# Weight slots handed on as they come free, turns amid the next pair's products, and the last two expert pairs combined on TensorE

## The reference, cut to what matters

```python
N_EXPERTS = 32; TOP_K = 2; D_EXPERT = 256; D = 1024      # 256 tokens

# router: one group of 8 experts per token, then the best two in it
w_top = softmax(top_logit) * p_grp
combine = one_hot(g_sel)[:, :, None] * w_exp[:, None, :]
for grp in range(4):                                      # 8 experts each
    hid = silu(einsum('td,edf->tef', t, w_gate[grp])) * einsum('td,edf->tef', t, w_up[grp])
    out = out + einsum('tef,efd->td', hid * combine[:, grp, :, None], w_down[grp])
h = h + m[5] * out
return rmsnorm(h, final_norm_g)
```

## Time and profile before

| | us |
|---|---|
| time, median of 3 runs | 2303.52 (2302.74 to 2309.55) |
| the profiled execution's own time | 2301.17 |
| its span | 2299.2 |
| PE busy in the span | 2061.1 (90%) |
| DVE busy | 787.0 (34%) |
| ACT busy | 500.0 (22%) |
| POOL busy | 125.1 (5%) |

### The profile page before, as it was taken

One profiled execution on the slowest core, in us unless ns is written; L12 is line 12 of the kernel. 1 busy time (PEld: TensorE's weight loads), 2 busy tenths in 40 slices (PEclk: granted clock), 3 DMA queues, 4 the chain that ended last, 5 costly groups with the idle time before them and its releaser, 6 DMA issues. The chain is left out here.

```text
span 2299.2 us, 35930 instructions
## 1 busy us (share of the span) xinstructions
PE 2061.1 (90%) x15698; PEld 1271.5 (55%) x15698; DVE 787.0 (34%) x1613; ACT 500.0 (22%) x1023; POOL 125.1 (5%) x127
## 2 busy tenths in 40 slices
PE   6989999999999999999998887899998996778874
PEld 3545568854445658864544786884498643322221
DVE  1474323211185323310244545436444412311112
ACT  2223321201114413210121332123332201211111
POOL 0000000000000000000000011000021000011111
PEclk9999999999999999999998888889989998899997
DMA  6351325533343236334211000100200262387873
GB/s 253 146 206 54 147 110 219 220 146 146 127 186 139 105 122 257 147 147 157 99 44 42 3 3 3 49 12 37 110 4 3 74 265 110 146 360 325 342 325 154
DMA packets 33978, 318.47 MB, mean 139 GB/s; under 512 B 7088, under 2 KB 9528, under 8 KB 12960
## 3 DMA queue, kind: packets, MB, share of 16 engines
q1 hardware_dynamic: 28064, 308.40, 34.1%
q0 software_dynamic: 5760, 7.78, 1.0%
HBM read 332.49 MB, written 13.65 MB: 151 GB/s over the span
## 5 line engine op out<-in xcount | busy, mean ns | idle before, releaser
L516 ACT ACTIVATE arena<-pair 128x512 f32<-128x512 f32 (+5 forms) x339 | 181.0, 547 | 694.7 <-PE pair L890 172.7
L1267 PE MATMUL pair<-arena,weight_ring 128*128 128x256 f32 x1408 | 311.0, 383 | 2.9 <-ACT arena L790 2.9
L890 PE MATMUL pair<-weight_ring,arena 128*128 128x512 f32 (+1 forms) x640 | 279.2, 590 | 19.2 <-issue 11.4
L1267 PEld LDWEIGHTS pair<-arena,weight_ring 128*128 128x128 f32 x1408 | 270.0, 192 | 43.9 <-issue 6.8
L890 PEld LDWEIGHTS pair<-weight_ring,arena 128*128 128x128 f32 x640 | 123.5, 196 | 157.2 <-issue 151.9
L1313 PE MATMUL pair<-weight_ring,arena 128*128 128x512 f32 x352 | 151.5, 592 | 3.1 <-DVE arena L1287 3.1
L1287 DVE SCALAR_TENSOR_TENSOR arena<-pair,columns,arena 128x255 f32<-128x255 f32 (+1 forms) x176 | 76.8, 478 | 202.3 <-ACT arena L1278 200.7
L2777 PE MATMUL pair<-arena 128*64 128x512 f32 x352 | 111.5, 651 | 24.8 <-DMA arena<-experts_in 24.8
L2777 PE MATMUL pair<-weight_ring,arena 128*64 128x512 f32 x288 | 96.1, 657 | 22.9 <-DMA weight_ring<-experts_in 18.4
L1313 PEld LDWEIGHTS pair<-weight_ring,arena 128*128 128x128 f32 x352 | 66.8, 190 | 86.7 <-issue 83.2
L1573 PEld LDWEIGHTS pair<-arena 64*64 64x64 f32 x3584 | 111.1, 139 | 3.6 <-issue 2.9
(11 more groups left out here) (487 smaller groups left out, 2580.2 us busy)
## 6 DMA issues: line engine op xcount, KB each, us to landing
weight_ring<-stream SPq DMA_DIRECT2D x85, 2048.0 KB, 7.3
arena<-experts_in SPq DMA_DIRECT2D x18, 2048.0 KB, 13.2
weight_ring<-experts_in SPq DMA_DIRECT2D x14, 2048.0 KB, 12.4
arena<-experts_out SPq DMA_DIRECT2D x8, 2048.0 KB, 14.2
weight_ring<-experts_out SPq DMA_DIRECT2D x8, 2048.0 KB, 15.4
weight_ring<-stream SPq DMA_DIRECT2D x4, 1024.0 KB, 4.7
arena<-rows_in SPq DMA_DIRECT2D x1, 3264.0 KB, 21.9
weight_ring<-stream SPq DMA_DIRECT2D x2, 1152.0 KB, 5.5
```

Source lines behind the costliest of these rows:

```text
L516: copy_act = lambda dst, src: nc.scalar.activation(dst, src, ACT_F.Copy)
L890: last = mm(bank[b][:, 0:n], hT[:, k, m * P:(m + 1) * P], w[:, k * n:k * n + n], start=(j == 0), stop=(j == KD - 1))
L1267: last = mm(bank[b][:, j * S:(j + 1) * S], w[:, at:at + P], hT[:, k, :], start=(k == 0), stop=(k == KD - 1))
```

## The change

- **Slots.** The loads are put in an order of fetching (by g, those of extra pairs 1.5 later), the slots in the order in which they are freed, and the two are matched: the next slot that comes free takes the next load in that order.
- **Turns.** Pair i-1's turns on PE stand after six of the eight k-blocks of pair i's gate and up products instead of behind them. On ACT its silu and the copy of the turned values stand ahead of the copy of the next window.
- **The last two pairs.** Their rows are not written to DRAM. DVE makes for each token tile and each of the two pairs a 128 x 128 matrix that holds the router's weight where a token's row lies in that pair, PE turns the four (after pair 1's down products), and at the end eight products with the pairs' scaled rows give their part of the sum; DVE adds it to the residual. The gathers of tokens whose rows lie in those pairs point at a row of zeros, and wait only for pair 17's write; the DRAM tensor is filled with zeros beforehand, by two DMAs on SP.

Cut to its core, the diff is:

```diff
-            expert_count = []
-            for g in range(3 * npairs):
-                if pair_windows[g // 3] < N_EXP:
-                    earlier = [f for f in range(g % NEXP_SLOT, g, NEXP_SLOT) if pair_windows[f // 3] < N_EXP]
-                    expert_count.append(16 * len(earlier) + 16)
+            freed = [0, 1] + [3 * i + j for i in range(1, npairs) for j in (0, 1, -1)] + [3 * npairs - 1]
+            is_extra = [pair_windows[g // 3] >= N_EXP for g in range(3 * npairs)]
+            fetched = sorted(range(3 * npairs), key=lambda g: g + 1.5 * is_extra[g])
+            next_fetch = dict(zip(freed, fetched[NEXP_SLOT:]))
+            slot_of = {g: n for n, g in enumerate(fetched[:NEXP_SLOT])}
+            for g in freed:
+                if g in next_fetch:
+                    slot_of[next_fetch[g]] = slot_of[g]
+            expert_count = {}
+            for n, g in enumerate(fetched):
+                if is_extra[g]:
+                    expert_count[g] = 32 if g % 3 == 2 else 16
                 else:
-                    expert_count.append(32 if g % 3 == 2 else 16)
+                    earlier = [f for f in fetched[:n] if slot_of[f] == slot_of[g] and not is_extra[f]]
+                    expert_count[g] = 16 * len(earlier) + 16
 
             def load_expert(g, mark=None):
 
-                if g >= 3 * npairs:
+                if g is None:
                     return
                 w = pair_windows[g // 3]
-                full = expert_full[g % NEXP_SLOT] if w < N_EXP else extra_full[3 * ((w - N_EXP) // 2) + g % 3]
-                slot = expert_slots[g % NEXP_SLOT]
+                full = expert_full[slot_of[g]] if w < N_EXP else extra_full[3 * ((w - N_EXP) // 2) + g % 3]
+                slot = expert_slots[slot_of[g]]
                 if w < N_EXP:
                     if SP:
                         if mark:
...
@@ -2592,6 +2601,11 @@
             expert8, start8, any8 = get(8), get(8), get(8)
             rows8 = get(8)
             firsts, limits = get(40), get(40)
+            late_at, late_ok, late_to = get(2, 2, TT), get(2, TT), get(2, TT)
+            late_zero = tT.rearrange("p a b -> p (a b)")[:, old_t.at:old_t.at + D]
+            late_of = [old_t(2, P) for _ in range(TT)]
+            late_q = [old_t(2, P) for _ in range(TT)]
+            lateT = old_ya(2, S)
             row_at, row_ok, row_spare = get(20), get(20), get(1)
 
             def first_max(dst, src, n, top):
@@ -2680,8 +2694,14 @@
                 if eng:
                     settle(eng)
             if POOL:
+                nc.gpsimd.memset(late_zero, 0.0)
                 nc.gpsimd.memset(sorted_x[:, :, 512:512 + CH], 0.0).then_inc(pool_done, 1)
             c.pool += 1
+            if SP:
+                SP.wait_ge(pool_done, c.pool)
+                SP.dma_start(y_dram[0:2 * S, :].rearrange("(r p) d -> p r d", p=P),
+                             late_zero.unsqueeze(1).to_broadcast([P, 4, D])).then_inc(zero_rows, 16)
+                SP.dma_start(y_dram[2 * S:2 * S + 17, :], late_zero[0:17, :]).then_inc(zero_rows, 16)
 
             def windows():
                 numbers = k3c("index", 8).unsqueeze(2).to_broadcast([P, 8, N_EXP])
@@ -2738,8 +2758,40 @@
                 link(nc.vector.scalar_tensor_tensor(row_at, row_at, row_spare, row_ok, ALU.subtract, ALU.mult))
                 link(nc.vector.tensor_scalar(row_at, row_at, row_spare, None, ALU.add))
                 nc.vector.tensor_copy(places_i[:, 0:20], row_at)
-                return nc.vector.tensor_copy(places_i[:, 20:24], place2.rearrange("p c m -> p (c m)"))
+                first = P * (pair_windows[npairs - 2] // 2)
+                nc.vector.tensor_scalar(late_ok, slots2, float(first + 2 * P), None, ALU.is_ge)
+                nc.vector.tensor_scalar(late_at[:, 0], slots2, -float(first), None, ALU.add)
+                link(nc.vector.tensor_scalar(late_at[:, 1], slots2, -float(first + P), None, ALU.add))
+                link(nc.vector.scalar_tensor_tensor(late_ok, slots2, float(first), late_ok, ALU.is_ge, ALU.subtract))
+                link(nc.vector.tensor_scalar(late_to, place2, -1.0, 2.0 * S + 16, ALU.mult, ALU.add))
+                link(tt(late_to, late_to, late_ok, ALU.mult))
+                link(tt(late_to, late_to, place2, ALU.add))
+                return nc.vector.tensor_copy(places_i[:, 20:24], late_to.rearrange("p c m -> p (c m)"))
             places_mark = dve_after(sorted_rows, ("dve", c.dve))
+            def late_pairs():
+
+                if DVE:
+                    DVE.wait_ge(zero_rows, 32)
+
+                def weights_of():
+                    for m in range(TT):
+                        for u in range(2):
+                            for q, into in ((0, late_of[m]), (1, late_q[m])):
+                                last = nc.vector.tensor_scalar(into[:, u, :], k3c("iota", P), late_at[:, u, q, m:m + 1],
+                                                               w12[:, q, m:m + 1], ALU.is_equal, ALU.mult)
+                        link(last)
+                        last = tt(late_of[m], late_of[m], late_q[m], ALU.add)
+                    return last
+                m_w = dve_after(weights_of, places_mark)
+
+                def turned():
+                    for u in range(2):
+                        for m in range(TT):
+                            last = nc.tensor.transpose(bank[6][:, S * u + P * m:S * u + P * m + P], late_of[m][:, u, :], ident)
+                    return last
+                p = pe_after(turned, m_w)
+                return act_after(lambda: copy_act(lateT.rearrange("p u s -> p (u s)"), bank[6][:, :]), p)
+
             for b in range(8):
                 take(b)
 
@@ -2765,22 +2817,29 @@
 
             def expert_inputs(i):
 
-                gu = bank[i % 2]
+                gu, turned = bank[i % 2], 6
                 if PE:
                     PE.wait_ge(act_done, window_copied[i])
                     if i >= 2:
                         PE.wait_ge(act_done, hidden_done[i - 2])
                 ws = [await_expert(3 * i + j) for j in range(2)]
                 if PE:
-                    for k in range(KD):
+                    for k in range(turned):
+                        for j in range(2):
+                            mm(gu[CH * j:CH * j + CH, :], xg[i % 2][:, k, j, :], ws[j][:, 512 * k:512 * k + 512],
+                               start=(k == 0), stop=False)
+                if i:
+                    turn_hidden(i - 1)
+                if PE:
+                    for k in range(turned, KD):
                         for j in range(2):
                             last = mm(gu[CH * j:CH * j + CH, :], xg[i % 2][:, k, j, :], ws[j][:, 512 * k:512 * k + 512],
-                                      start=(k == 0), stop=(k == KD - 1))
+                                      start=False, stop=(k == KD - 1))
                     last.then_inc(pe_done, 1)
                 c.pe += 1
                 inputs_done[i] = c.pe
                 for j in range(2):
-                    load_expert(3 * i + j + NEXP_SLOT, ("pe", inputs_done[i]))
+                    load_expert(next_fetch.get(3 * i + j), ("pe", inputs_done[i]))
 
             def hidden(i):
 
@@ -2798,6 +2857,10 @@
                     tt(h[:, 1, :], gu[:, 256:512], h[:, 0, :], ALU.mult).then_inc(dve_done, 1)
                 c.dve += 1
                 product_done[i] = c.dve
+
+            def turn_hidden(i):
+
+                gu, h = bank[i % 2], hs_[i % 2]
                 if PE:
                     PE.wait_ge(dve_done, product_done[i])
                     for t in range(2):
@@ -2832,7 +2895,7 @@
                     last.then_inc(pe_done, 1)
                 c.pe += 1
                 outputs_done[i] = c.pe
-                load_expert(3 * i + 2 + NEXP_SLOT, ("pe", outputs_done[i]))
+                load_expert(next_fetch.get(3 * i + 2), ("pe", outputs_done[i]))
                 if DVE:
                     DVE.wait_ge(pe_done, outputs_done[i])
                     if i >= 2:
@@ -2848,6 +2911,8 @@
                 at = pair_windows[i] // 2
                 if POOL:
                     POOL.wait_ge(dve_done, rows_done[i])
+                    if i == 0:
+                        POOL.wait_ge(zero_rows, 32)
                     if i:
                         POOL.wait_ge(y_sent, 16 * i)
                     POOL.indirect_dma_start(out=y_dram, out_offset=bass.IndirectOffsetOnAxis(ap=places_i[:, at:at + 1], axis=0),
@@ -2857,26 +2922,45 @@
             open_window(0)
             open_window(1)
             for i in range(npairs + 1):
+                if i:
+                    hidden(i - 1)
                 if i < npairs:
                     expert_inputs(i)
+                else:
+                    turn_hidden(i - 1)
                 if 1 <= i < npairs - 1:
                     open_window(i + 1)
                 if 1 <= i <= npairs:
-                    hidden(i - 1)
-                if 1 <= i <= npairs:
```

(38 more changed lines are left out.)

## The result

The changed kernel takes 2278.76 us (median of 4 runs, 2276.14 to 2282.1) against 2303.31 for the kernel before (4 runs beside it): ratio 0.9888, 95% interval 0.9867 to 0.991. It is faster by 24.5 us; the forecast was 2251, with a range of 2240 to 2266. The profiled execution has a span of 2274.2 us at a mean clock of 0.948.

What follows compares the result with a forecast made beforehand. Bound: TensorE waits for weight loads because extra pairs hold three of seven slots and the queue runs dry. Saving 44.3 us up to the last down products plus 7.7 at the end gives 52.0: 2251 us, range 2240 to 2266.

Steps and rivals of the forecast that it cites:

- two terms of a round: Expert loop, pair 4's products' end to pair 8's: load releases and load steps, 47.7 us, 49.6 with a slow start; three rounds 148.9.
- the price of a load: Weight-load queue: one 2.10 MB load costs 5.2 us in a full queue; six such steps, 31.2 us, in a round.
- The last stretch: From pair 16's products' end to the last down products: TensorE sets the pace, 42.8 us against 52.1 before.
- the end alone: Rival: loads cost more in a never-empty queue, the new order gives nothing, only 7.7 - 1.2 remain; 2297 us; chance 0.04.
- Start: Expert stage's start: pair 4 starts at 2030.4, its load 5.2 us earlier; its wait hides TensorE's hold for late weights.
- Slow starts: TensorE's slow clock after weight waits at pairs 4, 8, 12, 16: 1.9 us on three, half on the fourth, 6.7.
- The end: After the last down products: gathers hidden, late products under the additions, 9.4 us left on DVE; 7.7 saved.
- DVE's seven instructions: DVE ahead of the first window copy: seven instructions at 0.18 us, 1.3 us, move the whole stage.
- Turns: Turns amid the next pair's products: lose 0.4 us a round where loads decide, gain 3 x 0.47 where TensorE does.
- Row writes: Rival: POOL's row writes, one pair at a time, become the pace above about 11 us; slower, 2325 us; chance 0.03.
- signs of being wrong: Expert stage: waits at pairs behind extra ones (6, 10, 14), DVE's scaling waiting for rows sent, additions waiting for gathers.
- signs of being right: No 12 us queue gaps, one 3 to 5 us wait a round, rounds of 48 to 50, no copy waits but the last.

Runs made afterwards that it cites:

- the kernel with nothing fetched: Changed kernel with all 128 row numbers of weight fetches out of bounds for pairs without an expert, so nothing moves for them: 2256.7 us, ratio 0.9796.
- the late weights early: Changed kernel, nothing fetched for pairs without an expert, late pairs' weights made ahead of the loop and turned after pair 0's down products: 2255.0 us, ratio 0.9773.
- the one with late pairs alone: Kernel before plus only the last two pairs' new handling, with old slots and old turns: 2304.4 us, ratio 0.9987.
- the kernel with the 16 rows spread: Changed kernel with an extra pair's 16 fetched rows on partitions 0, 4, ..., 60 instead of 0 to 15: 2262.7 us, ratio 0.9827.

## Why the prediction was wrong

Its direction was right and its size was not: 24.5 us for 52. What the new order of loads does was right too, as the kernel with nothing fetched shows; what was missed is what the extra pairs' own fetches do to it.

- **The failed step** is that these fetches were put at nothing, in two terms of a round. The first lets the loads in pair 5's slots start "after pair 5's products, +3.68 + 7.25 = +10.9", with no wait for pair 5's own rows. Pair 4's products ended at 2040.2 and pair 5's at 2060.0, 19.8 later: it waited 5.95 us for its rows, and its first 24 matmuls took 8.02 for 5.16. That is the whole excess of the first round, 58.5 for 49.6; from there to pair 8's end it took the 38.7 forecast. The second is the price of a load, "So one load costs 5.2 us in a full queue": beside fetches it was 5.6, and loads landed late. In the later rounds TensorE waited at pairs 11, 12, 15 and 16 (4.1, 1.5, 5.9 and 2.0 us), and for rows at pair 13 (1.1); they took 52.1 and 55.3, 2.5 and 5.7 too many. The last stretch took 51.8 for 42.8, since pair 17's rows (0.7) and pair 19's load (6.1), which lands at 2238.3, are late too: 9 more.
- **The sum.** Three rounds took 165.9 us for 148.9 forecast. With the last stretch that is 26 of the 27.6 us by which the last down products end later than forecast (2257.94 for 2230.3). With nothing fetched the rounds took 152.5 and the last stretch 43.9, so 21 of the 26 are the fetches'. A load then cost the 5.2 forecast, and part of the 4.7 left are slow starts (below): at pairs 8, 12 and 16 they were 7.6 together for 5.7.
- **What the rows could tell.** The stretch of the earlier trace rows at 0.97 and 399 GB/s, from which the 5.2 comes, holds only the first 0.23 MB of a fetch, at its very end; a dry gap would have shown q0 alone at 25.0% of the engines. The rival "the end alone" came near, with a load that "takes more when the queue is never empty", at 0.04. But that isn't the cause: full for 81 us and without fetches, the queue has the old price.
- **Start.** Pair 4's products ended at 2040.2 for 2038.7 forecast: +1.5. The hold for late weights ended at 2018.47 as worked out (2018.5), but the products behind it took 7.70 instead of 5.16 for 24 matmuls, in part at the slow clock. Hidden it was not quite; pair 4 had nothing to wait for.
- **Slow starts** of TensorE behind a wait: forecast 1.9 each. With nothing fetched, the 24 matmuls behind the hold for the late weights and behind the waits at pairs 8, 12 and 16 took 6.25, 8.12, 8.13 and 6.85, against 5.16 at full clock, so 1.1 to 3.0:

```profile
2025.56 6.25 PE pair L2830 x24
...
2086.69 8.12 PE pair L2830 x24
...
2137.87 8.13 PE pair L2830 x24
...
2188.23 6.85 PE pair L2830 x24
```

  The Trainium skill, "TensorE: Matmul & The Clock Gate", section "HAM oscillation — how this bites in real kernels", has each wait pay this. Here each of the four did, but not in every run. With the late weights early, the waits of 3.79 us at pair 8 and 3.87 at pair 12 cost 0.2:

```profile
2087.60:2093.00 5.40, 5.36 (x25) 2.02 (x26) 0.00 (x0) 0.00 (x0) 0.00 (x0) 1.00 1.05 433
2135.40:2140.80 5.40, 5.40 (x25) 2.03 (x26) 0.00 (x0) 0.00 (x0) 0.00 (x0) 1.00 1.06 432
```

  Behind them the granted clock stayed at 1.00 and 24 matmuls took 5.37, while a wait of 3.82 with nothing fetched was followed by 0.50 in a stretch as long, and by 8.13. So the measured price is that of some waits, not of each, as the prediction allowed for pair 4; what decides it stays open.
- **The end**: 8.3 saved for 7.7, gathers hidden, late products under the additions: right.
- **DVE's seven instructions** ahead of the first window: 1.2 us (1980.22 to 1981.45) for 1.3: right. **Turns** at nothing: right by the time (2255.6 for 2256.7).
- **Row writes** as the pace: their landings rose to 10.3 in the median and 18.2 at most (8.4 and 10.0 in the earlier trace rows), and POOL waited 82.4 us for them, but nothing waited for POOL's writes: DVE's scaling shows no such wait. It stayed a rival.
- Of the forecast's signs of being wrong, none came: no waits right behind the extra pairs, none for rows sent, none for gathers. What came were waits it had not listed, on the extra pairs' own rows and at pairs 11, 15 and 19. Of its signs of being right, the rounds of 48 to 50 us did not come.

## What to carry to other kernels

Before a gap in a queue is closed, look at what else runs in that gap, and at how many DMA engines it uses, not only at how many bytes. Here a transfer of 768 KB on four engines, nearly harmless in the gap, held back the full-width loads beside it: four of them cost 22 us, nearly three times what their bytes would. Read the queue's share of the engines in a stretch where it is alone; if the rows must come, choose partitions that spread them, which left 6 of the 22. And when a count of bytes seems harmless, ask whether the work is wanted at all: here it was for places that nobody reads, and in the changed kernel leaving it out was worth nearly as much as the whole change.

## What was not expected

The same kernel varies by more than its interval suggests. The kernel before gave 2297.2 to 2317.9 over 15 runs beside one set of experiments, and profiles differ in when TensorE's clock falls to its lower level in a dense stretch long before the expert stage. Windows from 1250 on, of the kernel before and of the one with late pairs alone:

```profile
1250.00:1280.00 30.00, 25.86 (x589) 22.16 (x591) 14.14 (x22) 11.85 (x21) 2.66 (x3) 0.97 0.01 3
```

```profile
1250.00:1280.00 30.00, 25.85 (x442) 21.72 (x442) 11.06 (x18) 9.39 (x17) 0.00 (x0) 0.75 0.01 2
```

In the same 30 us one ran 589 matmuls at a granted clock of 0.97, the other 442 at 0.75; the changed kernel stands between (548 at 0.84). The code of that stretch is the same. It is not all that differs: the kernel with the 16 rows spread ran 587 there at 0.96, and yet its expert stage began at 1990.19, 8.6 us later than in the kernel before. Since such differences move all that follows, I read the effects of the parts from the stage's own length, one execution each, where the whole time did not tell them apart. What sets the clock's phase stays open.
